# Applying only the adaLN scale before head 0, and its shift during head 0's projections

## The reference

```
mod = silu(c) @ w_ada + b_ada            # c_ctx for context tokens, c for latent ones
shift, scale, gate = split(mod, 3)
h = rms_norm(x, norm_w)
h = h * (1 + scale) + shift
rq, rk, rv, rg, hq, hf_f, hf_b, hi, hg = split(h @ w_in, 9)   # w_in: 2048 x 9216
... retention on rq, rk, rv; HGRN2 on hq, sigmoid(hf_f), sigmoid(hf_b), hi ...
out = concat(o_r * silu(rg), o_h * silu(hg)) @ w_out
x = x + gate * out ;  y = rms_norm(x, final_norm_w)
```

## Time and profile before

| | us |
|---|---|
| median of 3 runs | 1489.44 |
| the profiled execution's own time | 1488.71 |
| its span in the trace | 1486.9 |
| PE busy | 1430.7 (96%) |
| DVE busy | 863.2 (58%) |
| ACT busy | 489.7 (33%) |
| POOL busy | 374.4 (25%) |
| DMA, mean | 132 GB/s |

### The profile page before, as it was taken

One profiled execution on the slowest core, in us unless ns is written; L12 is line 12 of the kernel. 1 busy time (PEld: TensorE's weight loads), 2 busy tenths in 40 slices (PEclk: granted clock), 3 DMA queues, 4 the chain that ended last, 5 costly groups with the idle time before them and its releaser, 6 DMA issues.

```text
span 1486.9 us, 26346 instructions
## 1 busy us (share of the span) xinstructions
PE 1430.7 (96%) x10868; PEld 1255.1 (84%) x10868; DVE 863.2 (58%) x1141; ACT 489.7 (33%) x850; POOL 374.4 (25%) x292
## 2 busy tenths in 40 slices
PE   2889999999999999999999999999999999999996
PEld 1467689988998899889988998999899988788884
DVE  6532347565666665666576556666675658632346
ACT  4323124323333333333323332333243234321234
POOL 0000011532062216221621261135114415301220
PEclk9899999999999999999999999999999999999998
DMA  8996922322232222221313131322222237264236
GB/s 352 422 398 254 348 90 69 103 72 91 66 107 58 92 77 95 75 89 64 107 61 107 47 121 47 106 81 87 89 81 81 84 119 257 72 219 149 86 114 226
DMA packets 65732, 195.63 MB, mean 132 GB/s; under 512 B 7888, under 2 KB 16336, under 8 KB 58336
## 3 DMA queue, kind: packets, MB, share of 16 engines
q1 hardware_dynamic: 65632, 194.12, 37.6%
HBM read 173.36 MB, written 16.53 MB: 128 GB/s over the span
## 4 chain that ended last, share of the span: by engine, by line
PE 89%; DMA 6%; DVE 2%; ACT 1%; POOL 0%; issue 0%; SPq 0%; DVEq 0%; ACTq 0%
PE ps L1674 35%; PE ps L1694 10%; PE ps L1696 10%; PE ps L1695 10%; DMA area<-in_w_mod 4%; PE ps L1868 4%; PE ps L1870 4%; PE ps L1869 4%; PE ps L1710 2%; PE ps L1616 2%; DMA area<-in_w_gate 1%; PE ps L1593 1%; PE ps L1654 1%; PE ps L1721 1%; DMA area<-in_w_out 1%; PE ps L1732 0%
## 5 line engine op out<-in xcount | busy, mean ns | idle before, releaser
L1056 DVE TENSOR_TENSOR w_lo<-area,w_hi 128x1024 fp32r<-128x1024 f32 x144 | 186.2, 1294 | 419.2 <-ACT w_hi L616 419.2
L616 ACT ACTIVATE w_hi<-area 128x1024 fp32r<-128x1024 f32 x144 | 152.5, 1059 | 594.0 <-PE ps L1696 302.5
L1674 PE MATMUL ps<-hT_hi,w_hi 128*128 128x320 f32 x1184 | 275.9, 314 | 0.0
L1674 PE MATMUL ps<-hT_hi,w_lo 128*128 128x320 f32 x1184 | 269.7, 309 | 0.0
L1674 PE MATMUL ps<-hT_lo,w_hi 128*128 128x320 f32 x1184 | 269.7, 309 | 0.0
L1694 PE MATMUL ps<-w_hi,hT_hi 128*128 128x512 f32 x640 | 253.9, 397 | 0.0
L1696 PE MATMUL ps<-w_hi,hT_lo 128*128 128x512 f32 x640 | 249.6, 390 | 0.0
L1695 PE MATMUL ps<-w_lo,hT_hi 128*128 128x512 f32 x640 | 249.2, 389 | 0.0
L1674 PEld LDWEIGHTS ps<-hT_hi,w_hi 128*128 128x128 f32 x1184 | 196.0, 188 | 4.8 <-issue 1.7
L1674 PEld LDWEIGHTS ps<-hT_lo,w_hi 128*128 128x128 f32 x1184 | 198.0, 188 | 0.0
L1674 PEld LDWEIGHTS ps<-hT_hi,w_lo 128*128 128x128 f32 x1184 | 198.0, 188 | 0.0
(11 more groups left out here) (232 smaller groups left out, 1837.3 us busy)
## 6 DMA issues: line engine op xcount, KB each, us to landing
area<-in_w_in SPq DMA_DIRECT2D x144, 512.0 KB, 3.6
area<-in_w_mod SPq DMA_DIRECT2D x32, 1024.0 KB, 9.4
area<-in_w_out SPq DMA_DIRECT2D x40, 512.0 KB, 3.6
area<-in_w_gate SPq DMA_DIRECT2D x16, 1024.0 KB, 7.3
area<-in_x_columns SPq DMA_DIRECT2D x4, 1280.0 KB, 9.7
o_hi_scratch<-area SPq DMA_DIRECT2D x14, 320.0 KB, 2.2
o_lo_scratch<-area SPq DMA_DIRECT2D x14, 320.0 KB, 2.6
hT_hi<-o_hi_scratch SPq DMA_DIRECT2D x14, 320.0 KB, 6.8
```

The lines of the kernel that those rows point to most:

```text
L616: act.activation(w_hi[:, n % 2, :], raw[:, n % 3, :], ACT.Copy).then_inc(wt_hi.sem, 1)
L1056: v.tensor_tensor(w_lo[:, n % 2, :], raw[:, n % 3, :], w_hi[:, n % 2, :].bitcast(F32), ALU.subtract).then_inc(wt_lo.sem, 1)
L1674: ins = mm(out[s], wt[:, n % 2, w], x[:, k, s * HALF:(s + 1) * HALF], start=k == 0 and step == 0, stop=k == KT - 1 and step == 2)
```

## The change

Modulation is loaded in eight groups of four 1 MB chunks: four with the scale of a quarter each, then four with the shift. Each chunk is now 16 matmuls of 128 columns. Slices are formed as x * (scale * norm_w) * rstd in one DVE operation for each class of tokens. After group 0, PE interleaves groups 1 to 4 with `ahead`. Groups 5 to 7 stand between the slices of chunks 6 to 8, and five loads of 1 MB (`w_first`, head 0's columns of the five column-major parts once more) between those of chunk 9: `correction` multiplies them by the shift. The result is turned to columns `corr` and added to rq, rk, both gates' arguments and hq by ACT (`corrected`). While chunks 9 to 16 run, DVE and ACT add the shift to `hT_hi` and `hT_lo`, slice by slice, for the token-major parts and the other heads. The gate's 16 loads are used in pairs, two pairs in each of chunks 10 to 13. The small loads, the decay constants, the rotary swap and the store of the gate move to later places. All that is computed stays.

```
-ADA_GROUPS = 4
+QUARTERS = 4
+ADA_GROUPS = 2 * QUARTERS
-ADA_ROWS = 2
+ADA_ROWS = 4
-GATE_FIRST, GATE_EACH = UNITS, 3
+GATE_FIRST, GATE_LAST = 10, 13
...
 SP
-                    sp.wait_ge(a_used.sem, a_used.at(ADA_CHUNKS - GATE_SLOTS + slot))
+                    sp.wait_ge(a_used.sem, a_used.at(ADA_CHUNKS + 1 + slot))
+                if prev is None and n in (11, 12, 13, 14):
+                    for k in {11: range(3, 5), 12: range(5, 9), 13: range(9, 13), 14: range(13, KT)}[n]:
+                        load_gate(k)
-                if n == 9 and h is not None:
+                if n == (12 if prev is None else 9) and h is not None:
+                    if prev is None:
+                        sp.wait_ge(r_fixed.sem, r_fixed.at(0))
...
-            units = {2: 0, 4: 1, 11: 2, 19: 3, 22: 4, 27: 5}
+            load(0, 0)
+            chunks = {3: 1, 6: 2, 9: 3, 12: 4, 14: 5, 17: 6, 20: 7, 24: 8, 28: 9, 32: 10, 36: 11}
...
 ACT
+            def high_input(k):
+                act.wait_ge(h_mod.sem, h_mod.at(k))
+                act.activation(hT_hi[:, k, :], x_in[:, k, :], ACT.Copy).then_inc(h_hi.sem, 1)
+            def corrected(h):
+                act.wait_ge(corr_ready.sem, corr_ready.at(0))
...
+                for s in range(2):
+                    for w, tokens in CLASSES:
+                        i = act.activation(KL[:, s, tokens], KL[:, s, tokens], ACT.Exp, bias=corr[:, 2 + s, w:w + 1], scale=-1.0)
+                    i.then_inc(z_exp.sem, 1)
...
 DVE
+            for quarter in range(QUARTERS):
+                modulation(quarter)
+                first, end = quarter * ADA_K, (quarter + 1) * ADA_K
+                scaled_input(first)
+                for k in range(first, end):
+                    if k + 1 < end:
+                        scaled_input(k + 1)
+                    low_input(k)
+                    if k == ADA_K + 1:
+                        split(0, 2)
+                split(0, (1, 3, 4, 5)[quarter])
...
+            def shifted_input(k):
+                dve.wait_ge(wt_used.sem, wt_used.at(0, COLUMN_CHUNKS - 1 + k // KC))
...
+                for w, tokens in CLASSES:
+                    i = v.scalar_tensor_tensor(out=shifting[k % 2][:, tokens], in0=hT_hi[:, k, tokens].bitcast(F32),
+                                               scalar=shift[:, k, w:w + 1], in1=hT_lo[:, k, tokens].bitcast(F32),
+                                               op0=ALU.add, op1=ALU.add)
...
+                    if 5 <= n < 9:
+                        modulation(n - 1)
+                    if n == 10:
+                        correction_columns()
+                    if 9 <= n < 16:
+                        shifted(shifted_slices(n))
+                    if n == 9:
+                        correction_rows()
...
 PE
+            for group in range(1, QUARTERS + 1):
+                c0, s0 = group * GROUP_CHUNKS, (group - 1) * AHEAD
+                ahead(s0, range(0, 2))
+                ada_chunk(c0)
+                ahead(s0, range(2, 4))
+                ada_chunk(c0 + 1)
+                ada_chunk(c0 + 2)
+                ahead(s0 + 1, range(0, 2))
+                ada_chunk(c0 + 3)
+                ahead(s0 + 1, range(2, 3))
+                modulation_columns(group)
+                ahead(s0 + 1, range(3, 4))
+                ahead(s0 + 2)
...
+                for k in range(KT):
+                    rows = slice(k % 4 * QUAD, (k % 4 + 1) * QUAD)
+                    ins = mm(out[rows, :], shift[:, k, :], ada_raw[:, slot, tile_cols(k)], start=k < 4, stop=k >= KT - 4)
...
+            def between_slices(n, j):
+                if n > UNITS and j == 0:
+                    modulation_columns(n - 2)
+                if n < COLUMN_CHUNKS - 1:
+                    ada_chunk((n - 1) * GROUP_CHUNKS + j)
+                elif j >= 2:
+                    correction(2 * j - 4)
+                    correction(2 * j - 3)
...
 PE, in token_chunk
+                if first_head(h):
+                    pe.wait_ge(s_lo.sem, s_lo.at(2 * j + 1))
...
+                    if first_head(h) and j == 0 and at == 1:
+                        correction_transposes()
+                    if first_head(h) and n <= GATE_LAST and at in (1, TILES - 1):
+                        for kg in range(2):
+                            gate_chunk(4 * (n - GATE_FIRST) + at // 2 + kg)
```

More of the change, by code:

```diff
@@ L62 @@
 ADA_SLOTS = 4
[L63 removed]
+ADA_TILE = ADA_COLS // 4
 AHEAD = 3
@@ L207, in layer @@
         nw = vecT[:, 2 * KT:3 * KT]
-        R0 = M0 + 3 * WIDE
-        var, rstd, newt = (area[:, R0 + j * T - WIDE // 4:R0 + (j + 1) * T - WIDE // 4] for j in range(3))
-        assert M0 + 2 * WIDE + ADA_TILE + 3 * KT <= R0 - WIDE // 4 and R0 + 3 * T - WIDE // 4 <= AREA
+        R0 = M0 + 2 * WIDE + ADA_TILE + 3 * KT
+        var, rstd, newt = (area[:, R0 + j * T:R0 + (j + 1) * T] for j in range(3))
+        shift = var[:, 0:KT * QUAD].rearrange("p (k m) -> p k m", k=KT)
+        shifting = (newt, rstd)
+        corr_row = o_two
+        assert R0 + 3 * T <= AREA
         gates = area[:, RET0:RET0 + 2 * D_MODEL].rearrange("p (s n) -> p s n", s=2)
@@ L367, in token_bank, with mods_known, shifted_slices @@
             return BB if t == 0 else t - 1
-        def gate_chunks(n):
-            first = (n - GATE_FIRST) * GATE_EACH
-            return range(first, min(first + GATE_EACH, KT)) if n >= GATE_FIRST and first < KT else range(0)
+        def mods_known(group):
+            return 2 * (group + 1) if group < QUARTERS else group + 1 + QUARTERS
+        def shifted_slices(n):
+            return range(4) if n == 9 else range(2 * n - 16, 2 * n - 14) if 10 <= n < 16 else range(0)
+        CLASSES = ((0, slice(0, P)), (1, slice(P, T)))
         block = ctx.enter_context(nc.Block())
@@ new lines, in _ @@
+            split(0, 0)
+            act.wait_ge(rstd_steps.sem, rstd_steps.at(0, 1))
+            act.activation(rstd, var, ACT.Ln).then_inc(rstd_act.sem, 1)
+            act.wait_ge(rstd_act.sem, rstd_act.at(0))
+            act.activation(rstd, rstd, ACT.Exp, scale=-0.5).then_inc(rstd_act.sem, 1)
+            for quarter in range(QUARTERS):
+                for k in range(quarter * ADA_K, (quarter + 1) * ADA_K):
+                    high_input(k)
+                    if k == ADA_K + 1:
+                        split(0, 2)
+                split(0, (1, 3, 4, 5)[quarter])
@@ L788, in items @@
                     act.activation(halves(new_queries(h)), part(h, 4), ACT.Copy).then_inc(h_q.sem, 1)
-                if n == 11:
+                if prev is None:
+                    for k in shifted_slices(n):
+                        high_shifted(k)
+                if n == 10 and prev is None:
+                    corrected(h)
+                if n == 11 and prev is not None:
                     act.wait_ge(h_q.sem, h_q.at(h))
@@ L1036, in modulation @@
-                mod_step(i)
+                    columns = ps[:, bank, w:ADA_TILE:QUAD]
+                    if group < QUARTERS:
+                        i = v.tensor_tensor(mods[:, w, ks], columns, bias_cols[:, 1, ks], ALU.add)
+                    else:
+                        i = v.tensor_tensor(shift[:, ks, w], columns, bias_cols[:, 0, ks], ALU.add)
+                mod_step(i)
+                if group < QUARTERS:
+                    for w in range(2):
+                        i = v.scalar_tensor_tensor(out=mods[:, w, ks], in0=mods[:, w, ks], scalar=1.0, in1=nw[:, ks],
+                                                   op0=ALU.add, op1=ALU.mult)
+                    mod_step(i)
@@ L1599, in modulation_columns @@
                 pe.wait_ge(row_out.sem, row_out.at(group))
-                for j in range(2):
-                    i = nc.tensor.transpose(ps[:, ada_bank(group), tile_cols(j)], mod_row[:, tile_cols(j)], ident)
-                i.then_inc(row_tr.sem, 1)
+                nc.tensor.transpose(ps[:, ada_bank(group), 0:P], mod_row, ident).then_inc(row_tr.sem, 1)
             def ahead(s, kks=range(ADA_K)):
@@ new lines, in correction_transposes @@
+            def correction_transposes():
+                pe.wait_ge(corr_rows.sem, corr_rows.at(0))
+                for i in range(CORRECTIONS):
+                    ins = mm(ps[:, C, i * QUAD:(i + 1) * QUAD], corr_row[:, tile_cols(i)], sel, start=True, stop=True)
+                ins.then_inc(corr_out.sem, 1)
+            def between_slices(n, j):
[6 more added lines that the diff above has]
+                    correction(2 * j - 3)
```

267 lines of the change are left out of this document (141 added, 126 removed).

## The result

The changed kernel takes 1494.11 us (median of 8 runs, 1493.01 to 1498.34), the kernel before beside it on the same chip 1490.73 us (8 runs). The ratio is 1.0031, with a 95% interval of 1.0019 to 1.0042: slower by 0.3%, where I forecast 1485.4 and faster, and above my range. The profiled execution has a span of 1492.1 us, 5.2 more than before where I had 4.0 less; 9.2 us are to be explained.

A forecast was written before the change was run, and what follows sets the result against it. Bound by data supply to 127.4 us, then by PE. T14 at 200.6, minus 28.8 for T6, plus 15.2 of work and 9.6 of waits, gives 196.6, 4.0 earlier: 1484.7, median 1485.4; range 1479.0 to 1491.5.

The forecast's parts named there:

- T14: End of chunk 13, 200.6 us before the change; forecast 196.6, 4.0 us earlier.
- T6: End of `ahead`, 127.4 us before the change; forecast 98.6, 28.8 us earlier.
- rival (d): Chunk 10: PE finds `s_lo` or `corr_rows` not ready, 5 to 8 us once, 1492; chance 0.07.
- my signs of being wrong: T6 after 103, narrow chunk above 1.3, gate waits under 5 or over 13, stretch behind T14 changed over 2 us.
- Chunks 6 to 13: Forecast section on PE's work: chunks 6 to 8 33.4 us, chunk 9 12.0, chunks 10 to 13 43.0.
- What is late next: Forecast section on PE's waits for gate data behind chunk 9: 9.6 us, bounds 0, 6.9 and 14.
- T9: End of chunk 8, forecast at 132.0 us.
- in pairs at 0.95: Chunks 10 to 13: 16 gate products in pairs at 0.95 us each, 15.2 us.
- Rival (c): Modulation and correction chunks: narrower matmuls not free, 1.0 us more a chunk, 19.4 later, 1508.8; chance 0.05.
- the walk: Buffer-by-buffer estimate of PE's waits for the last correction and gate loads: 8.4 us, plus 1.2 for shared engines.
- T10: End of chunk 9, where chunks 10 to 13 begin.
- (a): Rival: gate loads land in time or nearly, 1475.8 us, with half of the waits 1480.6; chance 0.13.

The follow-up runs named there:

- the two faster ones: The changed kernel with gate loads 3 to 15 cut to 64 columns, 1484.38 us, and the one with demand spread and the swap issued by ACT, 1485.81 us.
- the kernel with small gate loads: Changed kernel with gate loads 3 to 15 cut from 2048 to 64 columns: 1484.38 us, ratio 0.9959 to the kernel before.
- the demand spread: Changed kernel, five modulation chunks per `ahead` group, corrections and gate products earlier, constants early: 1491.60 us with the swap on SP behind gate load 11, 1485.81 on ACT.
- five chunks a group: Changed kernel with five modulation chunks per `ahead` group, gate products over chunks 9 to 13, constants early, swap on SP behind gate load 11: 1491.60 us.
- the chunks in a row: Changed kernel with the four modulation chunks of each of chunks 6 to 8 put behind the chunk's last slice: 1498.85 us, ratio 1.0057.

## Why the prediction was wrong

**The frame held.** The end moves with T14 (1287.0 to 1287.5 us behind it in the changed kernel and in the two faster ones, 1286.3 before; the 0.9 is within the 2 us I allowed). T6 came within 1.1 us, the first matmul within 0.3. In T6 there is some luck: the joints between wide and narrow matmuls are missing from it too (twelve places, 2.4 us), and half clock cost 2.9 (5.7 us of it behind the first slice) where I charged 2.2, against slices that I priced 0.91 and that take 0.88 (48 of them, 1.4 us less). DVE and ACT hid the shift, the swap wasn't late for its reader, and rival (d) didn't come: no wait for `s_lo` or `corr_rows`. None of my signs of being wrong came either: T6 below 103, a narrow chunk at 1.01, the waits at 8.0, the stretch behind T14 changed by 0.9. The list had no sign for PE's own time in a stage or for the rate of the DMAs, which is where the forecast went wrong.

**The failed step is the sum for chunks 10 to 13, PE's 43.0 in "Chunks 6 to 13" and the 9.6 in "What is late next": 52.6 us, measured 56.9**, and with it chunks 6 to 9, 45.4, measured 48.4. From T9 on I had 64.6 us with an upper bound of 69, three buffers each turned round at 3.8 us a load; measured are 69.5. I took the middle, and what came was the upper bound. By the kernel with small gate loads the 9.2 us of span are:

- PE's own work, 5.3 us: 2.0 up to T9, 0.5 in chunk 9, 2.8 in chunks 10 to 13. The term "12 modulation chunks at 1.0" left out 0.2 us at each insertion (12 x 0.2 = 2.4 in chunks 6 to 8), "in pairs at 0.95" measured 1.06 a gate product, and the transposes at 0.6 took 1.2. The triple that I took 0.9 from the earlier trace rows is read from the first start of its matmuls, so that the loss before it isn't in it, and it has one pair of joints for three products; the changed kernel has one for two. Rival (c) asked whether the narrow form is dearer and was answered no: 32 passes in 1.01 us, 32 ns each. The Trainium skill's 81 ns ("TensorE: Matmul & The Clock Gate", section on the back-to-back issue gap) isn't what these passes took, whose stationary operand has 32 columns. I had asked for the price of the matmul, not for that of the change between forms.
- The supply, 11.1 instead of 9.6: 1.5 us. The waits alone are 8.0, near my 8.4 + 1.2; the 3 us of half clock behind them have no term in the walk. The stage moved 373 GB/s, not 422, which over 56.9 us is 2.8 MB less. About 0.9 MB of it (2.3 us at 401) go missing beside the swap, at 323 and 292 GB/s, and about 0.8 MB at 190 to 195 us, at 236, when PE had yet to give buffers back. My 52.1 us for the bytes are 58.9 at 373, and the lower bound of T9 + 61.9 becomes T9 + 68.7, against T9 + 69.5 measured. That is a description and no proof: 373 is the mean that came about with those holes in it, not a ceiling.
- Before T10, 1.5 us: 0.3 at the first matmul, about 1.1 by half clock that lasted longer behind it; the rest is small.
- The stage behind T14, 0.9 us. Its cause is open.

The split is one order of subtraction. In the changed kernel PE and the loads wait for each other in turn, so what PE's own 3.3 us from T9 on would be worth by themselves no run shows. That they alone don't lose the gain is shown: with small gate loads the kernel has them all and takes 1484.4, and with the demand spread it has as many narrow products and takes 1485.8.

**The range.** All the misses of whole stages had one sign. I counted the waits' bounds (6.9 to 14) but let 88.4 us of PE's work stand with a bound for the narrow form alone; 4.5% on it was the forecast's whole gain. (The lower end, 1479.0, is called half of (a), which gives 1480.6; nothing hangs on it.) The trace of before showed the swap's dip too, 357 and 347 GB/s from 150 to 160 us at a share of 1.02, and I read the swap only as issuing time.

**Not settled.** How much of the 11.1 us is the swap's traffic and how much late buffers isn't parted: moving it never gained here, but no kernel ran without it, and none with a fourth gate buffer. Nor was the spreading of the demand run by itself: the constants and the swap moved with it, though those two moves gained nothing alone (1493.6, 1495.0 and, together, 1494.6).

## What to carry to other kernels

Moving work out of a stage that is short of data only pays if the stage that receives it isn't made short in turn: sum bytes over time for each stage after the move, and level them before anything else. Giving the swap to ACT, 11 us earlier, gained nothing while the demand was uneven (1494.1 and 1494.4 us) and over 5 us once it was level (1491.6 and 1485.8). Price the joints between two forms of matmul as well as the matmuls, and where many small terms add up to a stage, give the sum a bound.

## What the runs showed of the hardware

- A run of 128-column fp32 matmuls put between wide fp32r ones costs 0.2 us at its two joints; a pair of gate products between tile matmuls costs 0.3. In a row 32 passes cost 0.92 us, alone 1.01.
- PE ran at 1.2 GHz for 3.4 us behind waits of 2.29 and 3.49 us in the changed kernel, and for 6.8 us behind one of 3.70 with five chunks a group. The length of the wait alone doesn't tell: behind a wait of 1.64 us (the swap behind gate load 12) and one of 2.16 (the chunks in a row) the clock stayed full, and behind one of 1.44 with others shortly before it (the chunks in a row) it fell. Bridging the waits with matmuls that do nothing kept 2.4 GHz and gained nothing where the data were the limit. With the demand spread and the gate loads nearly done, 6.8 us of half clock went with a stage 2.6 us longer than its waits account for.
- Eight SBUF to SBUF DMAs of 64 KB take their engine 5.1 to 5.8 us to issue. With them in flight the rate falls although the DMA engines' share stays near 1.0: from 401 to 323 and 292 GB/s when SP issues them, from 421 to 383 and 325 when ACT does. The Trainium skill ("DMA: Bandwidth & Descriptors", section on why small descriptors are slow) says that transfers within SBUF don't suffer the penalty of small descriptors; here the rate of the transfers together fell all the same, and no run shows why.
